# Compression network's first layer of a two-block transformer kernel: split operands and single-pass matmuls

## The chip, the cores and the metric

The kernel runs on one NeuronCore of a Trainium2 chip. Its engines are TensorE (PE: matmuls; PEld: its weight loads), VectorE (DVE), ScalarE (ACT), GpSimd (POOL) and SyncE (SP, which issues most of the DMAs). Each works through its own list of instructions in order, and semaphores tie the lists together. The metric is device time in microseconds of one execution, given as the median of several runs. The profile's clock of the trace starts at the span's start; all times below of the form 383.3 are on it.

## What is computed

Two blocks of a transformer in float32 on 512 tokens of width 1024: a hybrid attention layer, then a layer with "native sparse attention", a gated MLP mixer and a feed-forward part. The change touches one piece of the second block, the network that compresses keys and values:

```python
def compress_tokens(t, pos_emb, w1, w2):            # t [B,G,S,dh], w1 [2048, 256], w2 [256, 64]
    ...
    chunks = t.reshape(B, G, n_chunks, CMP_STRIDE, dh)
    blocks = jnp.concatenate([chunks[:, :, i:i + n_cmp] for i in range(r)], axis=3)
    blocks = (blocks + pos_emb).reshape(B, G, n_cmp, CMP_BLOCK * dh)
    return jax.nn.gelu(blocks @ w1) @ w2
...
kc = compress_tokens(heads_kv(k_c), cmp_pos_k, cmp_w1_k, cmp_w2_k)
vc = compress_tokens(heads_kv(v_c), cmp_pos_v, cmp_w1_v, cmp_w2_v)
```

`blocks` has 2 groups x 31 blocks, held as 64 rows, of 32 x 64 = 2048 numbers. The product `blocks @ w1` (64 x 2048 by 2048 x 256), done once for the keys and once for the values, is "the first layer". The result feeds one of three attention branches of the second block.

## The kernel before

**Precision.** A float32 matmul is done by TensorE in several passes. The large products avoid this: each operand is split into a high part (rounded to the type `float32r`, copied by ScalarE) and a low part (the operand minus its high part, subtracted by GpSimd or VectorE), and three single-pass matmuls high x high, high x low and low x high replace one float32 matmul. The weights of these products arrive in `RAW`, and their two parts go into a ring `WR` of six slots. For each slot, step `split`, ScalarE copies the high part (L1859), then GpSimd subtracts the low part in two halves (L2756). A split stands four slots ahead of the matmuls that use it. The first layer, in contrast, is done in plain float32: `blocks` (64 columns) is the stationary operand, a row block of `w1` (128 x 256) the moving one, 16 such products for the keys and 16 for the values, each in two halves of 8, the steps `hidden 0,0`, `hidden 0,1` (keys) and `hidden 1,0`, `hidden 1,1` (values).

**Stages around it.** The input product of the second block, `in2`, is done in five chunks of columns (408, 512, 384, 512, 512 wide). Each chunk takes 8 weight slots, and for each slot TensorE does four token tiles of three matmuls (L1360). Each token tile has its own PSUM bank, and the chunk's result is copied out of the four banks by ScalarE (tiles 0 and 2) and VectorE (tiles 1 and 3), both L1031, before the next chunk may write there. Between these matmuls stand small steps:

- `qt` (L1627): transposes of one token tile into the one PSUM bank `TR`. All users of `TR` share it, so each must wait until the one before has been copied out. `qt cmp` feeds `cmpT`, from which VectorE forms `blocks` with the position embedding added (L2510, 8 instructions); `qt q` feeds `qS` (ScalarE L1925, then VectorE L2350); `qt slc` transposes `k_nat` and feeds `kS_slc` (ScalarE L1931, VectorE L2365).
- `hidden` (L1753), whose result ScalarE turns through GELU into `hid_nat` (L2061); `hid_t` (L1762) transposes that through `TR` into `hidT` or `hidV`; `cmpkv` (L1770, L1773) is the second layer, from which VectorE forms `kcS` and `vbd` (L2529 to L2534); `CS` (L1784) are the first attention scores, which need them.

**Order.** The lists of all engines come from one timeline. It is written by `make_timeline` from the table `PLAN`, which says before which quarter of a weight slot (one token tile, three matmuls) a step may stand; `follows` names what must have gone before it, `lags` the least distance, and `rank` the order of steps due at the same quarter. Every engine takes from the timeline, in order, what is its own.

## Time and profile before

| | us |
|---|---|
| median of 3 runs (964.64 to 964.97) | 964.74 |
| the profiled execution | 964.92 |
| its span | 962.7 |
| TensorE busy | 946.2 (98%) |
| the four halves of the first layer on TensorE, 3.60 each | 14.4 |

The profiled execution's time lies 2.2 us over its span and 0.2 us over the median. The chain of waits gives TensorE 90% of the span. TensorE's granted clock is 1.00 (2.4 GHz) in the stages from 352 to 418.

### The profile page before, as it was taken

What the parts mean: (1) busy time and instruction counts of PE and PEld (TensorE: products, weight loads), DVE (VectorE), ACT (ScalarE), POOL (GpSimd) and SP (SyncE); (2) the same over time, 40 slices, a digit from 0 to 9 for tenths busy, and PEclk for the clock granted to TensorE, in tenths of its full rate; (3) what the DMA queues carried; (4) which work ended last, traced back from release to release, by engine and by line L of the source; (5) the groups of instructions that cost most, each with busy time, mean ns of one, the idle gap of its engine ahead of it and who ended that gap; (6) DMA issues with size and microseconds to landing.
All of it is one profiled execution on the core that took longest, in us unless ns stands there. A gap on an engine that the chain in (4) does not pass through costs nothing.

```text
span 962.7 us, 14693 instructions
## 1 busy us (share of the span) xinstructions
PE 946.2 (98%) x5579; PEld 823.8 (86%) x5579; DVE 569.4 (59%) x1083; ACT 419.7 (44%) x730; POOL 369.0 (38%) x442
## 2 busy tenths in 40 slices
PE   9999999999999999999999999999999999999997
PEld 8878887878888898688888888888999999988886
DVE  2764445388554356384558743888899999711114
ACT  5334325265555263345464633544444444433332
POOL 5771551246435454122223036597000000366561
PEclk9999999999999999999999999999999999999999
DMA  7374243112144252231211112226322442122312
GB/s 234 120 199 99 66 143 99 45 44 66 44 147 160 70 175 66 76 122 45 72 62 65 45 44 89 74 69 213 116 89 89 128 136 88 46 88 91 124 47 88
DMA packets 74758, 93.44 MB, mean 97 GB/s; under 512 B 15332, under 2 KB 53777, under 8 KB 74688
## 3 DMA queue, kind: packets, MB, share of 16 engines
q1 hardware_dynamic: 74256, 91.91, 29.9%
q8 instruction: 45, 0.74, 0.3%
q10 hardware_dynamic: 432, 0.59, 0.2%
q14 instruction: 25, 0.20, 0.1%
HBM read 90.09 MB, written 7.12 MB: 101 GB/s over the span
## 4 chain that ended last, share of the span: by engine, by line
PE 90%; DVE 4%; ACT 2%; issue 2%; DMA 1%; POOL 0%; SPq 0%; DVEq 0%; POOLq 0%; ACTq 0%
PE psum L1360 52%; PE psum L1421 17%; PE psum L1701 6%; PE psum L1661 4%; PE psum L1676 3%; PE psum L1753 1%; PE psum L1487 1%; PE psum L1627 1%; PE psum L1729 1%; PE psum L1743 1%; PE psum L1714 1%; DMA RAW<-in_w_in_dram 1%; PE psum L1640 1%; PE psum L1799 0%; DVE R L2730 0%
## 5 line engine op out<-in xcount | busy, mean ns | idle before, releaser
L1360 PE MATMUL psum<-WR,XT 128*128 128x512 f32 (+3 forms) x1620 | 390.5, 387 | 1.0 <-ACT R L1031 0.7
L2756 POOL TENSOR_TENSOR WR<-RAW,WR 128x256 fp32r<-128x256 f32 (+3 forms) x320 | 259.9, 841 | 321.0 <-ACT WR L1859 320.9
L1360 PEld LDWEIGHTS psum<-WR,XT 128*128 128x128 f32 x1620 | 285.9, 188 | 51.5 <-issue 4.1
L2756 POOL TENSOR_TENSOR WR<-RAW_B,WR 128x256 fp32r<-128x256 f32 x88 | 71.6, 837 | 202.7 <-ACT WR L1859 202.7
L1859 ACT ACTIVATE WR<-RAW 128x512 fp32r<-128x512 f32 (+3 forms) x160 | 93.4, 603 | 83.5 <-PE psum L1360 69.4
L1360 PE MATMUL psum<-WR,TT 128*128 128x512 f32 x528 | 119.9, 389 | 0.0
L1360 PEld LDWEIGHTS psum<-WR,TT 128*128 128x128 f32 x528 | 99.0, 188 | 20.5
L2034 ACT ACTIVATE prob<-prob,st 128x512 f32<-128x512 f32 (+2 forms) x112 | 58.4, 545 | 92.6 <-DVE st L2418 83.5
L1701 PEld LDWEIGHTS psum<-ones_up,probT 128*128 128x128 f32 x536 | 70.7, 191 | 7.1 <-issue 1.3
L1701 PE MATMUL psum<-ones_up,probT 128*128 128x128 f32 x536 | 72.7, 275 | 0.1
L1421 PE MATMUL psum<-TT,WR 128*128 128x256 f32 x576 | 71.7, 283 | 0.0
L1421 PEld LDWEIGHTS psum<-TT,WR 128*128 128x128 f32 x576 | 70.3, 192 | 0.0
L1360 PE MATMUL psum<-XT,WR 128*128 128x512 f32 (+1 forms) x324 | 67.4, 367 | 0.0
L2613 DVE TENSOR_TENSOR TT<-actT,TT 128x512 fp32r<-128x512 f32 x22 | 17.6, 801 | 84.2 <-ACT TT L2090 84.1
L1360 PEld LDWEIGHTS psum<-XT,WR 128*128 128x128 f32 x324 | 56.2, 188 | 10.1 <-DVE XT L2241 0.2
L1859 ACT ACTIVATE WR<-RAW_B 128x512 fp32r<-128x512 f32 x44 | 27.2, 630 | 70.3 <-PE psum L1360 67.8
L2793 POOL TENSOR_TENSOR st<-st 128x8 f32<-128x8 f32 (+2 forms) x27 | 32.5, 1204 | 65.4 <-DVE st L2316 28.9
L1421 PE MATMUL psum<-XT,WR 128*128 128x256 f32 x432 | 54.1, 283 | 0.0
L1421 PEld LDWEIGHTS psum<-XT,WR 128*128 128x128 f32 x432 | 52.9, 192 | 0.1
L1676 PE MATMUL psum<-ident_sb,prob 128*128 128x128 f32 x268 | 43.1, 276 | 1.9 <-DVE probT L1096 1.2
L1096 ACT ACTIVATE probT<-psum 128x512 f32<-128x512 f32 (+2 forms) x52 | 25.2, 485 | 36.0 <-PE psum L1676 35.8
L2241 DVE TENSOR_TENSOR XT<-psum,XT 128x512 fp32r<-128x512 f32 x32 | 21.0, 687 | 30.0 <-ACT XT L1915 30.0
(292 smaller groups left out, 1254.0 us busy)
## 6 DMA issues: line engine op xcount, KB each, us to landing
RAW<-in_w_gate_up_dram SPq DMA_DIRECT2D x28, 512.0 KB, 5.0
RAW<-in_w_in_dram SPq DMA_DIRECT2D x13, 1024.0 KB, 5.2
RAW_B<-in_w_down_dram SPq DMA_DIRECT2D x11, 1024.0 KB, 5.0
RAW<-in_w_out_dram SPq DMA_DIRECT2D x8, 1024.0 KB, 5.3
RAW_B<-in_w_gate_up_dram SPq DMA_DIRECT2D x16, 512.0 KB, 6.0
RAW<-in_w_in_dram SPq DMA_DIRECT2D x13, 512.0 KB, 4.9
rep_scratch<-rows_scratch SPq DMA_DIRECT2D x12, 320.0 KB, 6.6
RAW<-in_w_in_dram SPq DMA_DIRECT2D x4, 768.0 KB, 4.3
```

Source lines behind the costliest of these rows:

```text
L1096: (eng.activation(dst, src, ACT.Copy) if eng is nc.scalar else eng.tensor_copy(dst, src)).then_inc(tr_out, 1)
L1360: last = pe.matmul(outp, stationary(x), moving(y), start=start and n == 0, stop=stop and n == 2)
L1421: last = pe.matmul(bank[:, 256 * m:256 * m + 256], w[:, k, y, P * m:P * m + P], x_[:, k, z, :], start=fresh and (k, m, y, z) == (0, 0, 0, ...
L1661: last = pe.matmul(bank[:, col:col + m * P], q_of(name, h)[:, P * i:P * i + P], k_of(name, h, x)[:, P * j:P * (j + m)], start=x == 0, stop ...
L1676: last = pe.transpose(TR[:, P * q:P * q + P], buf[:, P * q:P * q + P], ident[:, :])
L1701: last = pe.matmul(OB[:, P * i:P * i + P].rearrange("p (x n) -> p x n", x=2), probT[:, at_:at_ + P], ones_and_v(name, h, j + b), start=b = ...
L1859: act.activation(WR[:, s % RING, 0, 0:w], (DOWN_RAW if s >= first["down", 0] else RAW)[:, raw_half[g], q, 0:w], ACT.Copy).then_inc(w_hi, 1)
L2034: last = act.activation(buf[:, col:col + m * P], buf[:, col:col + m * P], ACT.Exp, bias=nm[:, sl + n:sl + n + 1], scale=-1.0)
L2241: dve.tensor_tensor(XT[:, 4 * hf:4 * hf + 4, 1, P * t:P * t + P], (MM[i] if kind_ == "mm" else XB[i]).rearrange("p (q n) -> p q n", q=4), ...
L2613: dve.tensor_tensor(AT[:, kt % 8, 1, :], actT[:, kt, :], AT[:, kt % 8, 0, :].bitcast(F32), ALU.subtract).then_inc(act_lo, 1)
L2756: last = pool.tensor_tensor(WR[:, s % RING, 1, lo:hi], raw[:, raw_half[g], q, lo:hi], WR[:, s % RING, 0, lo:hi].bitcast(F32), ALU.subtract)
L2793: pool.tensor_tensor(dst, src, half[:, 0:1].broadcast_to([P, n]) if n > 1 else half[:, 0:1], ALU.pow).then_inc(r_ready, 1)
```

## The change

1. **Matmuls.** `blocks` is split too, into `block_parts[kv]` with 64 high and 64 low columns side by side: one stationary operand of 128 columns. Each row block of `w1` is split into `hi_of_w1` and `w1_lo`. For each of the 32 row blocks there are two single-pass matmuls, with the high and the low part of `w1` as the moving operand of 256 columns. PSUM rows 0 to 63 then hold the product with the high part of `blocks`, rows 64 to 127 the one with its low part.
2. **Adding the halves.** ScalarE copies rows 64 to 127 to `hid_nat`, VectorE adds rows 0 to 63, and ScalarE applies GELU. Before, ScalarE applied GELU straight from PSUM.
3. **Splitting `w1`.** 16 new steps `w1`, each for a pair of row blocks: ScalarE copies 128 x 512 high parts, GpSimd subtracts the low parts, in place over `w1`, in two pieces of 256 columns. Pairs 0 to 7 (keys) are due at quarters 16 to 37 of `in2`, pairs 8 to 15 (values) at quarters 62 to 69. Pair 8 and pair 10 wait until the first and the second half of `block_parts` are done, pair 12 until `hidden 0,0` is.
4. **Splitting `blocks`.** Two new steps `bp`: ScalarE copies 128 x 1024 high parts, VectorE subtracts. Keys and values signal apart.
5. **Places.** `hidden` moves from quarters 64, 65, 67, 69 to 64, 66, 69, 72; `hid_t` from 67, 72 to 69, 75; `qt cmp` from 41 to 39 and `blocks` from 55 to 53; `cmpkv` stays at 70, subject to what it follows. The keys' `w1` is now loaded first (in the place and at the time of the values' before), the values' second. Buffers are moved for the new tiles.

```diff
     if kind == "hidden":
         kv, part = at
-        return [("hidden", kv, 0)] if part else [("hidden", 0, 1)] if kv else [("blocks",)]
+        out = [("w1", 4 * (2 * kv + part) + 3)]
+        return out + ([("hidden", kv, 0)] if part else [("hidden", 0, 1)] if kv else [("blocks",), ("bp", 1)])
...
                     if part == 0:
                         wait_sc(step)
-                        pe.wait_ge(s_w1[kv], 16)
-                        pe.wait_ge(blk_done, 1)
+                        pe.wait_ge(blk_done, kv + 1)
+                    pe.wait_ge(w1_lo_done, 4 * (2 * kv + part) + 4)
                     for m in range(8 * part, 8 * part + 8):
-                        last = pe.matmul(SC[nth["hidden", kv, 0] % 2][0:64, 0:256], blocks[:, kv, m, :], w1[kv][:, m, :],
-                                         start=m == 0, stop=m == 15)
-                    if part:
-                        last.then_inc(sc_in, 1)
+                        for x, moving in enumerate((hi_of_w1(16 * kv + m), w1_lo[kv][:, m, :])):
+                            last = pe.matmul(SC[nth["hidden", kv, 0] % 2][:, 0:256], block_parts[kv][:, m, :, :].rearrange("p x n -> p (x n)"), moving,
+                                             start=(m, x) == (0, 0), stop=(m, x) == (15, 1))
+                    last.then_inc(sc_in if part else w1_used, 1)
...
+                elif what == "w1":
+
+                    pair = step[1]
+                    kv, m = divmod(2 * pair, 16)
+                    act.wait_ge(s_w1[kv], 16)
...
+                    if pair in (8, 10):
+                        act.wait_ge(blk_done, pair // 2 - 3)
+                    if pair == 12:
+                        act.wait_ge(w1_used, 1)
+                    act.activation(hi_of_pair(pair), w1[kv][:, m:m + 2, :], ACT.Copy).then_inc(w1_hi_done, 1)
...
                 elif what == "hidden" and step[2]:
                     kv = step[1]
                     act.wait_ge(sc_in, nth["hidden", kv, 0] + 1)
-                    if kv == 0:
-                        act.wait_ge(tr_in, nth["qt", "cmp", 3] + 1)
-                    act.activation(hid_nat[0:64, kv, :], SC[nth["hidden", kv, 0] % 2][0:64, 0:256], ACT.Gelu_apprx_tanh).then_inc(hid_act, 1)
+                    act.activation(hid_nat[0:64, kv, :], SC[nth["hidden", kv, 0] % 2][64:128, 0:256], ACT.Copy).then_inc(hid_low, 1)
+
+                    act.wait_ge(sc_out, nth["hidden", kv, 0] + 1)
+                    act.activation(hid_nat[0:64, kv, :], hid_nat[0:64, kv, :], ACT.Gelu_apprx_tanh).then_inc(hid_act, 1)
...
+                if what == "w1":
+                    pair = step[1]
+                    kv, m = divmod(2 * pair, 16)
+                    pool.wait_ge(w1_hi_done, pair + 1)
+                    for e in range(2):
+                        last = pool.tensor_tensor(w1_lo[kv][:, m + e, :], w1[kv][:, m + e, :], hi_of_pair(pair)[:, e, :].bitcast(F32), ALU.subtract)
+                    last.then_inc(w1_lo_done, 1)
```

The change moves instructions at three places that matter below (line numbers of the changed kernel are up to 59 higher).

ScalarE, end of chunk 0 of `in2`, before:

```order
L1859 ACTIVATE WR<-RAW 128x408
L1859 ACTIVATE WR<-RAW 128x512 x4
L1031 ACTIVATE cmp_nat<-psum,st 128x4x64
L1031 ACTIVATE k_nat<-psum,st 128x2x64
```

The same place after, where `w_hi_...<-w_k` are the copies of the pairs 0 to 5:

```order
L1889 ACTIVATE WR<-RAW 128x408
L2098 ACTIVATE w_hi_b<-w_k 128x512
L1889 ACTIVATE WR<-RAW 128x512
L2098 ACTIVATE w_hi_b<-w_k 128x512
L1889 ACTIVATE WR<-RAW 128x512
L2098 ACTIVATE w_hi_a<-w_k 128x512
L1889 ACTIVATE WR<-RAW 128x512
L2098 ACTIVATE w_hi_a<-w_k 128x512 x2
L1889 ACTIVATE WR<-RAW 128x512
L2098 ACTIVATE w_hi_a<-w_k 128x512
L1061 ACTIVATE cmp_nat<-psum,st 128x4x64
```

Six copies now stand ahead of the one that frees chunk 0's first PSUM bank (`cmp_nat`).

ScalarE, from the high part of the values' blocks to the third `qS`, before (`nat_92` frees a bank of chunk 1):

```order
L1031 ACTIVATE nat_92<-psum,st 128x512 x2
L1925 ACTIVATE qS<-psum 64x4x128 x2
L1859 ACTIVATE WR<-RAW 128x384
L1925 ACTIVATE qS<-psum 64x4x128 x2
L2061 ACT_TABLE_LOAD
L2061 ACTIVATE hid_nat<-psum 64x256
L1925 ACTIVATE qS<-psum 64x4x128 x2
```

The same place after:

```order
L2105 ACTIVATE block_parts_v<-blocks 128x16x64
L2098 ACTIVATE w_hi_d<-w_v 128x512 x2
L1061 ACTIVATE nat_92<-psum,st 128x512 x2
L1955 ACTIVATE qS<-psum 64x4x128 x2
...
L2098 ACTIVATE w_hi_a<-w_v 128x512
L2109 ACTIVATE hid_nat<-psum 64x256
L2112 ACT_TABLE_LOAD
L2112 ACTIVATE hid_nat<-hid_nat 64x256
L1955 ACTIVATE qS<-psum 64x4x128 x2
```

Three instructions came ahead of the bank's copy, and the table load, which stood ahead of the wait for TensorE, now stands behind the copy that has this wait.

TensorE, from the last half of the first layer to the first scores, before:

```order
L1627 MATMUL psum<-ident_sb,k_nat 128x128 x2
L1360 MATMUL psum<-WR,XT 128x384 x6
L1627 MATMUL psum<-ident_sb,k_nat 128x128 x2
L1360 MATMUL psum<-WR,XT 128x384 x3
L1762 MATMUL psum<-ident_sb,hid_nat 128x64 x2
L1360 MATMUL psum<-WR,XT 128x384 x6
L1770 MATMUL psum<-hidT,w2k 128x64 x2
L1773 MATMUL psum<-w2v,hidV 128x64 x4
L1360 MATMUL psum<-WR,XT 128x384 x3
L1627 MATMUL psum<-ident_sb,k_nat 128x128 x2
L1360 MATMUL psum<-WR,XT 128x384 x6
L1784 MATMUL psum<-kcS,qS 128x64 x8
```

The same place after (the first row is two steps of two transposes each, back to back):

```order
L1657 MATMUL psum<-ident_sb,k_nat 128x128 x4
L1390 MATMUL psum<-WR,XT 128x384 x9
L1657 MATMUL psum<-ident_sb,k_nat 128x128 x2
L1792 MATMUL psum<-ident_sb,hid_nat 128x64 x2
L1390 MATMUL psum<-WR,XT 128x384 x6
L1800 MATMUL psum<-hidT,w2k 128x64 x2
L1803 MATMUL psum<-w2v,hidV 128x64 x4
L1814 MATMUL psum<-kcS,qS 128x64 x8
```

The large matmuls that stood between steps which hand `TR` or `kcS` on to one another have moved away from between them.

## Rows read from the trace of the kernel before

**Rows 1.** The page: busy time, share of the span, instructions of each engine.

```profile
PE 946.2 (98%) x5579; PEld 823.8 (86%) x5579; DVE 569.4 (59%) x1083; ACT 419.7 (44%) x730; POOL 369.0 (38%) x442
```

**Rows 2.** Chain of waits, 330 to 430: start, us, what stands on the chain.

```profile
358.89 6.39 PE psum L1360 x27
...
382.86 0.44 PE psum L1627 x4
383.30 3.60 PE psum L1753 x16
...
404.35 0.39 ACT kS_slc L1931
404.84 0.43 DVE kS_slc L2365
...
405.65 1.26 PE psum L1360 x6
...
407.30 0.91 PE psum L1773 x8
...
410.57 1.06 PE psum L1784 x8
```

**Rows 3.** Chain of waits, 700 to 712, where single-pass matmuls of 256 columns run.

```profile
699.94 12.12 PE psum L1421 x101
```

**Rows 4.** Timeline of ScalarE, 346 to 364: start, duration, instruction [idle before, releaser].

```profile
352.37 2.66 ACT L1859 ACTIVATE WR<-RAW 128x408 fp32r<-128x408 f32 x5
357.20 0.47 ACT L1031 ACTIVATE cmp_nat<-psum,st 128x256 f32<-128x256 f32 x1 [2.16 <-PE psum L1360]
```

**Rows 5.** DMAs: issue of the second w1, and (all DMAs by line) its us to landing.

```profile
340.29 0.37 SPq L1267 DMA_DIRECT2D w_k<-in_cmp_w_k_dram  x1
...
w_k<-in_cmp_w_k_dram SPq DMA_DIRECT2D x1, 2048.0 KB, 9.9
```

**Rows 6.** Timeline of GpSimd, 300 to 400.

```profile
353.74 6.78 POOL L2756 TENSOR_TENSOR WR<-RAW,WR 128x204 fp32r<-128x204 f32 x10
...
374.90 1.15 POOL L2756 TENSOR_TENSOR WR<-RAW,WR 128x192 fp32r<-128x192 f32 x2 [2.04 <-ACT WR L1859]
378.11 1.39 POOL L2756 TENSOR_TENSOR WR<-RAW,WR 128x192 fp32r<-128x192 f32 x2 [2.06 <-ACT WR L1859]
```

**Rows 7.** Timeline of VectorE, 376 to 412: the blocks.

```profile
377.15 0.57 DVE L2510 TENSOR_TENSOR blocks<-cmpT,st 128x248 f32<-128x248 f32 x1
...
377.63 1.46 DVE L2510 TENSOR_TENSOR blocks<-cmpT,st 128x248 f32<-128x248 f32 x2
...
380.31 1.07 DVE L2510 TENSOR_TENSOR blocks<-cmpT,st 128x248 f32<-128x248 f32 x2
```

**Rows 8.** Groups by line and shape: count | busy us, mean ns | idle before.

```profile
L2674 DVE TENSOR_TENSOR WR<-formed,WR 128x1024 fp32r<-128x1024 f32 x24 | 29.3, 1222 | 5.3 <-ACT WR L1881 5.1
...
L1881 ACT ACTIVATE WR<-formed 128x1024 fp32r<-128x1024 f32 x24 | 25.4, 1059 | 22.9 <-PE psum L1421 13.7 <-PE psum L1360 8.0 <-DVE formed L2668 1.2
```

**Rows 9.** Timeline of all engines, 352 to 418: one `qS`, and the GELU of the keys.

```profile
382.22 0.69 ACT L1031 ACTIVATE nat<-psum,st 128x512 f32<-128x512 f32 x1 [0.67 <-PE psum L1360]
...
383.33 1.19 ACT L1925 ACTIVATE qS<-psum 64x512 fp32r<-64x512 f32 x2 [0.43 <-PE psum L1627]
...
384.63 1.39 DVE L2350 SCALAR_TENSOR_TENSOR qS<-psum,qS 64x512 fp32r<-64x512 f32 x2 [0.98 <-ACT qS L1925]
...
389.31 1.28 ACT L2061 ACT_TABLE_LOAD   x1
...
391.69 0.38 ACT L2061 ACTIVATE hid_nat<-psum 64x256 f32<-64x256 f32 x1 [1.10 <-PE psum L1753]
```

**Rows 10.** Waits, 376 to 416: engine, line, for whom: us, times, longest.

```profile
PE psum L1784 <- DVE vbd L2534: 0.5, 1, 0.5
PE psum L1762 <- DVE kS_slc L2365: 0.5, 1, 0.5
...
PEld psum L1627 <- DVE kS_slc L2365: 0.3, 1, 0.3
```

More of the change, by code:

```diff
@@ L301, in make_timeline @@
         "OS": 1.5, "CS_b": 1.5, "F": 2, "sp_b": 2.5, "S": 3, "Z": 3, "sp": 4, "qt": 4.5,
-        "gx": 4.2, "xt": 4.4, "blocks": 5, "hidden": 6, "hid_t": 6.5, "gelu": 6, "cmpkv": 7, "gm_w": 8, "gm_a": 9, "gm": 10,
+        "gx": 4.2, "xt": 4.4, "blocks": 5, "bp": 5.2, "w1": 5.5, "hidden": 6, "hid_t": 6.5, "gelu": 6, "cmpkv": 7, "gm_w": 8, "gm_a": 9, "gm": 10,
     }
@@ L461, in make_timeline @@
         on(PLAN["hidden"][n], ("hidden", n // 2, n % 2))
+    for n in range(2):
+        on(PLAN["bp"][n], ("bp", n))
+    for pair in range(16):
+        on(PLAN["w1"][pair], ("w1", pair))
     for n in range(2):
@@ L997, in ones_and_v, with hi_of_w1, hi_of_pair @@
             return ones_up[:, 0:2 * at_].rearrange("p (x n) -> p x n", x=2)[:, :, 0:HD]
+        def hi_of_w1(n):
+            part, slot = ((1, 0), (0, 0), (0, 4), (2, 0), (3, 0), (3, 4), (0, 0), (0, 4))[n // 4]
+            return w1_hi[part][:, slot + n % 4, :]
+        def hi_of_pair(pair):
+            part, slot = ((1, 0), (0, 0), (0, 4), (2, 0), (3, 0), (3, 4), (0, 0), (0, 4))[pair // 2]
+            return w1_hi[part][:, slot + 2 * pair % 4:slot + 2 * pair % 4 + 2, :]
         def bias_of(name, h, i, m):
@@ L1258, in load_w1 @@
             def load_w1(kv):
-                if kv:
+                if not kv:
                     sp.wait_ge(tr_in, nth["F", 3, 2] + 1)
```

51 lines of the change are left out of this document (41 added, 10 removed).

## Prediction

> **What bounds the kernel now.** I read the busy line first: TensorE is busy 98% of the span [rows 1], so what leaves TensorE's list gains, and what makes TensorE wait costs, nearly one for one. Then the chain of waits around the first layer [rows 2]: each of the four halves of the first layer (L1753 x16) is on it with 3.60 us, and between 403 and 411 it leaves TensorE for short handovers through VectorE and ScalarE. Then the timelines of the three engines to which the change gives work [rows 4, 6, 7, 9], for where they have room. Everything up to the end of chunk 0 of `in2` and everything after the scores keeps its order, so the difference arises between 353 and about 417.
>
> **What TensorE saves.** Before, 4 x 3.60 = 14.4 us. After, each half has 16 single-pass matmuls of 256 columns with a stationary operand of 128 columns. The same shape runs elsewhere at 12.12 / 101 = 0.120 us [rows 3], so a half takes 1.92 us: 4 x 1.68 = 6.7 us saved. The Trainium skill (TensorE: Matmul & The Clock Gate, "Back-to-back issue gap") gives N/2.4 + 2.5 ns, 109 ns for 256 columns; by it 0.7 us more would be saved, but the row has this kernel's own spacing, and the sum goes by that.
>
> **What the change adds, in order of the program.** Between engines I allow 0.06 us for each handover.
>
> (a) *ScalarE before chunk 1.* Before, ScalarE ends a burst of five copies at 355.0 (2.66 us, 0.53 each), then idles 2.16 us until chunk 0's first bank is full at 357.20 [rows 4]; TensorE's chunk 1 starts at 358.89, when that bank is copied out [rows 2]. Now six copies of `w1` pairs stand in this burst: 6 x 0.53 = 3.2 us against 2.16 idle. ScalarE reaches the bank 1.0 late, and TensorE with it: **+1.0** (0.8 to 1.3). The keys' `w1` is no wait here: even the second load, issued at 340.29, lands 9.9 us later [rows 5], and the keys' is now the first.
>
> (b) *ScalarE, then VectorE, in chunk 1.* Two more copies come ahead of the gates' exponential, which VectorE needs before it may empty `TR` after the first `qt cmp`; the second `qt cmp` then waits a little: **+0.3** (0 to 1.0). Chunk 1 now ends at 382.86 [rows 2] + 1.3 = 384.2.
>
> (c) *First `qt q`, behind the blocks.* Before, GpSimd is idle for most of the time in which VectorE forms the blocks; only one split lies beside them, at 378.11, and it stretches from 1.15 to 1.39 [rows 6], while the pair of blocks instructions at 377.63 takes 1.46 against 1.07 for the pair at 380.31 [rows 7]. With the pair after it, that one split costs VectorE 0.7 us. Now GpSimd has eight `w1` pairs at 2 x 0.71 = 1.42 (the burst from 353.74 has eight pieces of 256 columns and two of 204 in 6.78 [rows 6]), 11.4 us, and runs without a gap from 353.74: chunk 1's last split ends near 377.7, and four splits of chunk 2 follow, all beside the blocks. The blocks start at 377.1 again (1.3 later by a and b, 1.4 earlier since `qt cmp` stands two quarters ahead), take eight times 0.5 alone and 4 x 0.7 for the splits: done at 384.0. Then, in a row: VectorE's subtract for the keys, 1.22 [rows 8], for which pair 8 waits on ScalarE; two copies of pairs, 1.07; the copy of chunk 1's first bank, 0.69 [rows 9]; the transposes. That is 387.0 with handovers, against 384.2 when TensorE is there: **+2.8**. The ends: with one split beside the blocks, as before, they are done at 381.9 and the wait is 0.7; with VectorE at half speed all the time and a little more for its two subtracts, 3.6. I take 2.8 since the only rows with both engines at it say so. What is queued on VectorE behind this is the second bank of chunk 1, needed only after the first half of the layer.
>
> The Trainium skill (SBUF — State Buffer, "SBUF: two separate sides") has a rule against this change: GpSimd and a VectorE instruction with two SBUF inputs share one port pair, and who comes second is held for the other's whole instruction. Each of the eight GpSimd pieces would then hold VectorE by its full 0.575 instead of the 0.35 that the rows show: (c) would be 4.6 instead of 2.8 and the whole forecast 1.8 us later.
>
> (d) *Second `qt q`.* Its `TR` must be emptied: ScalarE 1.19, VectorE 1.39 [rows 9], 2.7 with handovers. TensorE has a half (1.92) and three matmuls (0.6) for it: **+0.2** (0 to 0.5).
>
> (e) *Fourth `qt q`.* Its list is now: second half for the keys, 3 matmuls, third `qt q`, 6 matmuls, fourth `qt q`, which waits until the third is out of `TR`. On ScalarE, ahead of emptying the third, stand the low rows' copy, which waits for that half, the table load and the GELU. From the half's end: 0.38 + 1.28 + 0.38 + 1.19 (ScalarE), 1.39 (VectorE) [rows 9], 4.8 with handovers. TensorE meanwhile has 9 matmuls of 384 columns (six take 1.26 [rows 2]), 1.9, and four transposes, 0.44: **+2.4** (1.8 to 2.8). Before, the table load was over at 390.6, before the half ended [rows 9].
>
> (f) *`hid_t` of the keys* waits for the fourth `qS`, 2.7, with only a half, 1.92, to cover it: **+0.8** (0.5 to 1.2).
>
> (g) *Two `qt slc` back to back* after the last half. The second waits until ScalarE has copied the low rows (0.38), VectorE has added (0.4), ScalarE has done GELU (0.38) and its part of `kS_slc` (0.39), and VectorE its part (0.43 [rows 2]): 2.3 with handovers, less the first one's own 0.4, 1.9. Six matmuls covered this before, and 0.3 was left [rows 10]: **+1.6** (1.2 to 1.9).
>
> (h) *`hid_t` of the values* directly behind the third `qt slc`: 0.39 + 0.43 and handovers, 1.0; before, three matmuls covered it and 0.5 was left [rows 10]: **+0.5** (0.3 to 0.7).
>
> (i) *First scores directly behind `cmpkv`.* From the end of `cmpkv` at 407.30 + 0.91 to the scores at 410.57 are 2.36 us of VectorE forming `kcS` and `vbd` [rows 2]. Before, nine matmuls and two transposes lay in them and 0.5 was left as a wait [rows 10]; now nothing lies there: **+1.8** (1.6 to 2.0).
>
> The GpSimd pieces themselves I cost at nothing on top: without contention, chunk 1's fourth slot is ready at 367.7 and needed at 369.5, its last at 377.7 and needed at 381.3. That cover is thin, and its loss is the rival B. The final order of the DMAs (the t5 biases follow the last half) moves with TensorE and is not waited for.
>
> **Sum.** -6.7 + 1.0 + 0.3 + 2.8 + 0.2 + 2.4 + 0.8 + 1.6 + 0.5 + 1.8 = **+4.7 us**. All low ends together give +0.2, all high ends +8.3. On the profiled execution's 964.92 that is 969.6, on the median, 0.2 less, **969.4**. So the single passes save what they promise, and more than that is spent in handovers whose covering matmuls have been thinned out.
>
> **Rivals.**
>
> *A: the saving shows (faster).* The waits (d) to (i) all hang on one point: that nothing stands between the emptying of `TR` and its next user. If TensorE's queue and the engines behind it close these gaps as they did before, when four `qt q` cost no wait at all, only (a), (b) and the low end of (c) remain: -6.7 + 1.0 + 0.3 + 0.7 = -4.7, 960.0. With (c) at 0.7, the kernel is faster by more than can be told from no change as soon as (d) to (i) together come to under 2.8 us. Before, the same handovers left 0.3 to 0.5 each [rows 10], which speaks for it; but there matmuls lay between, and the printed order has none. 0.08.
>
> *B: GpSimd falls behind (slower still).* If each piece costs GpSimd what the contended split shows (1.39 for 1.15, a fifth more [rows 6]), nine groups of pieces up to chunk 1's fourth slot bring 2.7 us and the slot comes 0.9 late; sixteen groups up to the last slot bring 4.8, and it comes 1.2 late; TensorE waits for `WR` in chunk 1. +4.7 + 1.2 = +5.9, 970.6. Most of that time VectorE works from PSUM, beside which the splits kept their pace, so 0.14.
>
> *C: half of it.* The blocks are not held up (c at 0.7) and (e) falls to half, since ScalarE's list is shorter than I make it: +1.4, 966.1, within 0.2%. 0.12.
>
> *D: the change does not do what it says,* that is, a matmul of 128 stationary and 256 moving columns here takes longer than 0.120, say the 0.225 of a sixteenth of a half before (3.60 / 16): no saving, and only (d) and (f), which a half covers, fall away: 11.4 - 1.0 = +10.4, 975.1. The same types and shape are in rows 3, so 0.02.
>
> **How the numbers follow.** The forecast gets 0.64, and its own range is 967.0 to 971.8. The range for 8 in 10 leaves out A and the upper end of B and D, and takes in most of C: 965.6 to 972.2. A measurement of this kernel can tell about 0.2%, 1.9 us, from no change: slower is above 966.7, faster below 962.8. Slower: the forecast, B, D and nothing of C, less a margin for terms that I may have counted twice, 0.78. Same: C and that margin, 0.13. Faster: 0.09.
>
> **What would show it.** In the profile of the changed kernel the halves should be 1.9 us each on the chain; chunk 1 should start near 359.9; TensorE should idle before the first `qt q` (2 to 3 us, behind VectorE's blocks instructions of 0.7 to 0.9 us instead of 0.57), before the fourth (2.4, VectorE's `qS`), before the second `k_nat` pair (1.9) and before the first scores (2.3). If the idle stands before L1390 with GpSimd as the releaser, it is B; if TensorE is still gapless, A. I am wrong outright if the chain shows fewer than 5 us of new waits between 353 and 417.

## The result, and the profile after

| | before | after |
|---|---|---|
| median, us | 964.86 | 987.52 (987.19 to 987.81) |
| profiled execution's span, us | 962.7 | 986.0 |
| TensorE busy, us | 946.2 (98%) | 949.3 (96%) |

The ratio is 1.0235, with a 95% interval of 1.0217 to 1.0253: the change makes the kernel 22.7 us slower. The direction was forecast, the size was not: 969.4 with a range up to 972.2. No rival comes near it either.

The page of the kernel after, its busy line (it answers to [rows 1]) and two lines of the span in 40 slices of 24.65 us:

```profile
PE 949.3 (96%) x5579; PEld 831.9 (84%) x5579; DVE 584.5 (59%) x1087; ACT 430.8 (44%) x750; POOL 392.8 (40%) x474
...
PE   9999999999999985789999999999999999999997
...
PEclk9999999999999997969999999999999999999999
```

TensorE is no longer busy throughout: four slices, from 345 to 444 us, show only some 80%, 50%, 70% and 80%, and in the second and the fourth of them the granted clock is well below full speed too. Its timeline there, with the idle time ahead of a row and who ended it in brackets (rows of the large product lie between):

```profile
359.82 4.55 PE L1390 MATMUL psum<-WR,XT 128*128 128x512 f32 x19 [0.94 <-ACT st L1061]
...
379.80 1.12 PE L1657 MATMUL psum<-ident_sb,cmp_nat 128*128 128x128 f32 x4 [11.76 <-DVE cmpT L2412]
380.57 4.15 PE L1390 MATMUL psum<-WR,XT 128*128 128x512 f32 x12
...
384.91 3.00 PE L1390 MATMUL psum<-WR,XT 128*128 128x512 f32 x12
...
397.98 0.63 PE L1657 MATMUL psum<-ident_sb,nat 128*128 128x128 f32 x4 [0.74 <-issue]
...
401.40 0.66 PE L1657 MATMUL psum<-ident_sb,nat 128*128 128x128 f32 x4 [0.34 <-DVE qS L2401]
...
409.40 0.66 PE L1657 MATMUL psum<-ident_sb,nat 128*128 128x128 f32 x4 [2.85 <-DVE qS L2401]
...
419.66 0.44 PE L1657 MATMUL psum<-ident_sb,k_nat 128*128 128x128 f32 x2 [2.09 <-DVE kS_slc L2416]
...
423.93 0.47 PE L1792 MATMUL psum<-ident_sb,hid_nat 64*128 64x64 f32 x2 [1.00 <-DVE kS_slc L2416]
...
431.45 1.89 PE L1814 MATMUL psum<-kcS,qS 128*128 128x64 f32 x8 [2.38 <-DVE vbd L2593]
```

The second line is half of the story: the second `qt cmp` waits 11.76 us. The first layer itself is as forecast where the clock is full: in the first half of the keys the 16 matmuls stand 0.120 us apart (398.69, 398.81, 398.93 and so on), 1.92 us. The third half, behind the wait of 2.85 us, takes 3.1. The releaser, VectorE's copy of `cmpT`, was not slow. It stood behind this:

```profile
364.88 12.31 DVE L2598 TENSOR_SCALAR st<-st 128x96 f32<-128x96 f32 x1 [3.96 <-ACT st L2128]
...
378.02 0.42 DVE L2409 COPY cmpT<-psum 64x256 f32<-64x256 f32 x1
```

L2598 adds 1 to 96 numbers per partition, a step on the way to the branch gates, and takes 12.31 us. GpSimd's timeline in that time, the first and the last of its rows:

```profile
363.39 2.82 POOL L2834 TENSOR_TENSOR w_k_lo<-w_k,w_hi_a 128x256 fp32r<-128x256 f32 x4
...
374.37 2.76 POOL L2815 TENSOR_TENSOR WR<-RAW,WR 128x256 fp32r<-128x256 f32 x4
```

GpSimd subtracts low parts from 353.87 without a pause, and its run ends at 377.13. VectorE's instruction ends at 377.19. The other half of the story is the clock. Stretches of the span: length, busy us (and number of instructions) of PE, PEld, DVE, ACT and POOL, granted clock, share and GB/s of the DMAs:

```profile
379.00:382.00 3.00, 2.20 (x8) 1.92 (x9) 1.75 (x5) 0.00 (x0) 0.00 (x0) 0.50 0.63 230
...
409.00:413.00 4.00, 3.60 (x20) 3.47 (x20) 1.72 (x3) 2.25 (x5) 4.00 (x7) 0.66 0.00 0
...
423.00:432.00 9.00, 5.70 (x23) 5.42 (x23) 3.30 (x12) 2.04 (x3) 1.14 (x2) 0.50 1.01 365
432.00:440.00 8.00, 8.00 (x40) 7.90 (x40) 4.04 (x11) 0.80 (x2) 0.00 (x0) 0.65 0.03 10
```

0.50 is the lower level, 1.2 GHz. Here it stands behind the longer waits: the first 12 matmuls behind the 11.76 us take 4.15 us, 12 of the same shape at 384.91 take 3.00.

**The account** of the 23.3 us of span: the eight waits above are 22.1 us, less 1.0 that stood at two of these places before [rows 10], less the 6.7 saved, is 14.4. The remaining 8.9 are put down to the clock. This is what is left over, not a measurement; an estimate bears it out: busy time times what is missing to 1.00, over the stretches from 379 to 440, is about 10 us (TensorE's busy time is not all bound by its clock). Up to 352 the stages of the two kernels agree, and the last 522.7 us have the same number of matmuls and 514.5 us of TensorE's work in both, so nothing was lost elsewhere.

### The profile page after: what moved, and what is told of

It reads as the page before. It is cut to its first block, busy times and chain, and to the rows that moved or that the text cites. A ratio compares the mean times of both kernels' runs of the same rounds, so it can differ in the third digit from the quotient of the medians.

```text
span 986.0 us, 14751 instructions
## 1 busy us (share of the span) xinstructions
PE 949.3 (96%) x5579; PEld 831.9 (84%) x5579; DVE 584.5 (59%) x1087; ACT 430.8 (44%) x750; POOL 392.8 (40%) x474
## 4 chain that ended last, share of the span: by engine, by line
PE 56%; DVE 4%; ACT 2%; issue 1%; POOL 0%; DVEq 0%; POOLq 0%; ACTq 0%
PE psum L1390 30%; PE psum L1451 16%; PE psum L1731 3%; PE psum L1691 2%; PE psum L1706 2%; DVE st L2598 1%; PE psum L1784 1%; PE psum L1657 1%; PE psum L1517 1%; DVE R L2789 0%; PE psum L1814 0%; DVE qS L2401 0%; PE psum L1846 0%; ACT WR L1889 0%; ACT w_hi_a L2098 0%
## 5 line engine op out<-in xcount | busy, mean ns | idle before, releaser
L1390 PE MATMUL psum<-WR,XT 128*128 128x512 f32 (+3 forms) x1620 | 394.7, 390 | 1.8 <-ACT st L1061 0.9
L1390 PEld LDWEIGHTS psum<-WR,XT 128*128 128x128 f32 x1620 | 289.6, 191 | 52.0 <-issue 4.1
```

The source lines that it names most:

```text
L1390: last = pe.matmul(outp, stationary(x), moving(y), start=start and n == 0, stop=stop and n == 2)
```

## The experiments

The kernel before was run beside each of them, with medians from 964.8 to 965.0. Where a kernel ran once, its one time is given. The executions of one changed kernel scatter by up to 7.1 us (e10) where those of before scatter by at most 0.7, so single microseconds are read from the profiled executions. "The +1" is L2598's addition; the letters (L, S, Q, R and so on) are the theories of the expectations.

**e1: a pause for VectorE.** GpSimd waits, ahead of pair 5, until the +1 is done.

```diff
                     link(dve.tensor_scalar(g_tmp, g_tmp, 1.0, None, ALU.add))
+                    dve.sem_inc(gates_added, 1)
...
                 if what == "w1":
...
+                    if pair == 5:
+                        pool.wait_ge(gates_added, 1)
```

> The changed kernel, but GpSimd waits, before the low parts of pair 5, until VectorE's addition for the gates (L2598 in the changed kernel, 12.31 us there) is done. Theory L (port): this one-input SBUF instruction is held for as long as GpSimd's subtractions follow one another without a pause, so it ends when GpSimd pauses at 367.6: 2.7 us instead of 12.3, the second `qt cmp` waits 2 us instead of 11.8, time 973 to 976. Theory D (VectorE's own): the 12.3 us come from something at VectorE or ScalarE and not from GpSimd's run; then GpSimd waits with it, and the time is 987 or more.

973.68 us. Timeline of VectorE, then of GpSimd:

```profile
364.51 2.80 DVE L2599 TENSOR_SCALAR st<-st 128x96 f32<-128x96 f32 x1 [3.96 <-ACT st L2129]
```

```profile
365.82 1.43 POOL L2817 TENSOR_TENSOR WR<-RAW,WR 128x256 fp32r<-128x256 f32 x2
367.52 1.41 POOL L2838 TENSOR_TENSOR w_k_lo<-w_k,w_hi_a 128x256 fp32r<-128x256 f32 x2 [0.27 <-DVEq L2600]
```

The +1 ends at 367.31, 0.06 behind the end of the piece ahead of the pause. A pause of 0.27 us is worth 13.8 us.

**e2: the +1 with two inputs.** The same value from an instruction that reads `g_tmp` twice, max(x + 1, x).

```diff
-                    link(dve.tensor_scalar(g_tmp, g_tmp, 1.0, None, ALU.add))
+                    link(dve.scalar_tensor_tensor(out=g_tmp, in0=g_tmp, scalar=1.0, in1=g_tmp, op0=ALU.add, op1=ALU.max))
```

> The changed kernel, but the addition for the gates is a form with two SBUF inputs (x+1 as max(x+1, x)) in place of one with one input. Theory L: forms with two SBUF inputs take turns with GpSimd (the blocks of the kernel before: 0.57 became 0.93), so it lasts under 1.5 us, and the time is what was forecast without this stall, 968 to 974. Rival L2: every VectorE instruction that needs SBUF beside GpSimd is held until the run ends: 12 us again, 987.

986.37 (983.38 to 987.88), ratio 1.0226 (1.0209 to 1.0243). Timeline of VectorE:

```profile
364.41 12.37 DVE L2598 SCALAR_TENSOR_TENSOR st<-st 128x96 f32<-128x96 f32 x1 [3.95 <-ACT st L2128]
```

Held as long, to 376.78, 0.12 behind GpSimd's end. One input from SBUF or two makes no difference for the +1, and the expected 968 to 974 fell.

**e3: no low parts for the keys.** GpSimd leaves the keys' eight pairs out, and the second matmul of each row block takes the high part again, so that TensorE's work is the same and the keys' first layer is computed with another operand.

```diff
+                    if pair < 8:
+                        pool.sem_inc(w1_lo_done, 1)
+                        continue
```

> The changed kernel without GpSimd's 16 subtractions for the keys (the second matmul of each row block takes the high part again, so the low part of the keys' weights is left out of the result; the number and shape of matmuls stay). Theory L: GpSimd pauses before and while the gates are added, the addition lasts under 1 us, time 967 to 973. Theory D: 12.3 us and 987, since ScalarE's copies and VectorE's list are unchanged.

971.09. Timeline of VectorE:

```profile
364.56 0.21 DVE L2598 TENSOR_SCALAR st<-st 128x96 f32<-128x96 f32 x1 [3.96 <-ACT st L2128]
```

0.21 us is what the +1 takes when it is let in at once. The second `qt cmp` waits for nothing, and 16.4 us are back. In the kernel before the same instruction took 0.73, beside pieces of GpSimd: the sign was there, in a trace that I had read for other lines. Timelines of VectorE, GpSimd and ScalarE of the kernel before:

```profile
363.10 0.73 DVE L2539 TENSOR_SCALAR st<-st 128x96 f32<-128x96 f32 x1 [2.31 <-ACT st L2077]
```

```profile
360.93 4.23 POOL L2756 TENSOR_TENSOR WR<-RAW,WR 128x256 fp32r<-128x256 f32 x6 [0.42 <-ACT WR L1859]
```

```profile
362.87 0.62 ACT L1859 ACTIVATE WR<-RAW 128x512 fp32r<-128x512 f32 x1
```

It ended at 363.83, inside a row of six pieces of 256 columns without a pause. "What stays open" returns to this.

**e4: the kernel before, low parts of chunk 1 in pieces of 64 columns**, eight to a split.

```diff
-                    for lo, hi in ((0, w // 4 * 2), (w // 4 * 2, w)):
+                    pieces = [(64 * e, 64 * e + 64) for e in range(8)] if first["in2", 1] <= s < first["in2", 1] + 8 else ((0, w // 4 * 2), (w // 4 * 2, w))
+                    for lo, hi in pieces:
```

> The kernel before, with nothing of the change, but GpSimd's splits of chunk 1 of `in2` in eight pieces of 64 columns instead of two of 256. A piece should cost 0.33 us (0.21 + 0.0019 per column, from pieces of 130 to 256 columns), a slot 2.7, and GpSimd then runs without a pause from 355 to about 376, while each slot is still ready before TensorE needs it. Theory L: the addition for the gates (0.73 us before) is held to about 376, 12 to 13 us, the kernel before becomes 12 to 18 us slower, 977 to 983. Theory D: 0.7 us and 965.

964.62: no loss. Timeline of GpSimd, then of VectorE:

```profile
353.89 22.57 POOL L2757 TENSOR_TENSOR WR<-RAW,WR 128x204 fp32r<-128x204 f32 x72
```

```profile
363.24 0.43 DVE L2539 TENSOR_SCALAR st<-st 128x96 f32<-128x96 f32 x1 [2.30 <-ACT st L2077]
```

GpSimd runs for 22.57 us without a pause, as after, and yet VectorE gets in within 0.43. An unbroken run alone is not the cause, and the expectation fell. Two things differ from the kernel after: the width of the pieces, and everything else that the change brought. The next two runs part them.

**e5 and e6: the kernel before, with nothing changed but more for GpSimd to do** in chunk 1, in pieces of 256 and of 128 columns. The extra low parts go into free memory. e5's lines are below; in e6 all pieces of chunk 1 have 128 columns, two extra and four real ones to a split.

```diff
+                    n = s - first["in2", 1]
...
+                    if 0 <= n < 8:
+                        for e in range(2):
+                            part, at_ = (0, 2 * n + e) if n < 4 else (1 + (n - 4) // 2, 2 * (n % 2) + e)
+                            pool.tensor_tensor(spare[part][:, at_, :], RAW[:, raw_half[g], q, 256 * e:256 * e + 256], WR[:, s % RING, 0, 256 * e:256 * e + 256].bitcast(F32), ALU.subtract)
```

> The kernel before, in which GpSimd subtracts each of the eight low parts of chunk 1 of the second projection twice, the extra one (two pieces of 256 columns, ahead of the real ones) into memory that nothing reads. No other engine has anything new to do, and TensorE's order is that of before. At 0.70 us a piece (the 6.78 for 10 of [rows 6]) the 32 pieces are 22.5 us, a run from about 354 to 376 us as in the kernel after, in pieces of the same width. Theory L (VectorE's +1 for the gates, which reads and writes SBUF, is held as long as GpSimd's pieces of 256 columns follow each other with no pause): the +1 takes over 8 us and up to 13, TensorE's second turn of the compression queries waits for it, and the time is 975 to 983. Rival M (the 12.31 us come from something else that the change brought: ScalarE's copies of the key weights, their transfer, or the places in memory): the +1 takes 0.4 to 1.5 us, and the time is 964 to 967, the most being what chunk 1 loses to low parts that come later.

> The same in pieces of 128 columns: per split of chunk 1 two extra ones ahead of four real ones, 48 in all. In the run with pieces of 64 columns a piece took 0.31 us, in [rows 6] one of 256 took 0.70, so one of 128 is estimated at 0.44 and the run at 21 us without a pause. Theory S (the width of a piece decides: where a piece is short enough, VectorE comes in at a boundary): either the +1 takes 0.4 to 1.0 us as with 64 columns, and the limit lies between 128 and 256, or it takes over 8 us, and the limit lies between 64 and 128. Rival Q (not the width, but whether the next piece stood ready already decides): here as with 64 columns all pieces of a split stand ready, so the +1 takes under 1 us here and over 8 us in the run with 256 columns only if the width matters too; a value between, of 2 to 6 us, would say that VectorE waits for the end of a split. Time 964 to 967 where it is short.

e5 978.33, e6 974.43. Timeline of VectorE in e5, of GpSimd in e5, of VectorE in e6 and of GpSimd in e6:

```profile
362.89 15.18 DVE L2540 TENSOR_SCALAR st<-st 128x96 f32<-128x96 f32 x1 [2.23 <-ACT st L2078]
```

```profile
375.51 2.48 POOL L2765 TENSOR_TENSOR WR<-RAW,WR 128x256 fp32r<-128x256 f32 x4
```

```profile
363.23 10.83 DVE L2540 TENSOR_SCALAR st<-st 128x96 f32<-128x96 f32 x1 [2.28 <-ACT st L2078]
```

```profile
373.44 2.85 POOL L2765 TENSOR_TENSOR WR<-RAW,WR 128x128 fp32r<-128x128 f32 x6
```

In e5 the +1 ends at 378.07, GpSimd's run at 377.99. Neither ScalarE's copies, nor the transfers, nor the places in memory, nor anything on TensorE is needed to hold VectorE for 15 us: rival M has fallen, and L stands for pieces of 256 columns. With 128 columns it is held too, though it was done at 374.06, 2.2 us ahead of the end of the run at 376.29, for a reason that no row shows. By the expectation the limit would lie between 64 and 128 columns; whether it is the width that decides is tested by e13 below.

**e7: the +1 on ScalarE.** GpSimd's run stays as it is.

```diff
                     act.activation(g_tmp, g_tmp, ACT.Exp, scale=-1.0).then_inc(gate_e, 1)
+                    act.wait_ge(gate_e, 1)
+                    act.activation(g_tmp, g_tmp, ACT.Copy, bias=1.0).then_inc(gate_e, 1)
...
-                    dve.wait_ge(gate_e, 1)
-                    link(dve.tensor_scalar(g_tmp, g_tmp, 1.0, None, ALU.add))
+                    dve.wait_ge(gate_e, 2)
```

> The kernel after with the gates' +1 taken from VectorE: ScalarE adds it behind its Exp (a Copy with bias 1), and VectorE has the reciprocal alone. GpSimd's run is as it was. Theory L1 (only some forms of VectorE's work on SBUF are held: the +1 was in all runs, the reciprocal of 0.75 us ran beside GpSimd in the kernel before): the reciprocal takes about 0.75 us at 365 to 366, the second turn of the compression queries waits for nothing, and the time is that of the run without low parts for the keys, 970.5 to 972.5. Rival L2 (every instruction of VectorE on SBUF alone is held): the reciprocal takes 11 to 12 us, and the time is 985 to 988.

974.08 (973.91 to 978.53), ratio 1.0111 (1.0087 to 1.0135). Timeline of VectorE, then of GpSimd:

```profile
364.85 0.75 DVE L2600 RECIPROCAL st<-st 128x96 f32<-128x96 f32 x1 [4.27 <-ACT st L2130]
...
376.41 4.29 DVE L2563 TENSOR_TENSOR blocks<-cmpT,st 128x248 f32<-128x248 f32 x1
```

```profile
374.14 6.18 POOL L2816 TENSOR_TENSOR WR<-RAW,WR 128x256 fp32r<-128x256 f32 x10
```

The reciprocal, SBUF to SBUF in the middle of GpSimd's run, takes its 0.75 us: not every instruction is held, L2 has fallen for it. But the time missed the expected 970.5 to 972.5, because a second victim came up. GpSimd's run now ends at 380.32, and the first addition of the blocks, 0.57 alone [rows 7], is held to 380.70. The first `qt q` waits 4.13 us: its row names no releaser, but ScalarE reaches the copies of chunk 1's banks only at 386.82, behind its work on the blocks and the pairs. In the kernel after this was hidden, since everything but GpSimd was 12 us late by then.

**e10: three pairs of key weights behind the blocks** instead of ahead of them, on top of e7.

```diff
-'w1': (16, 19, 22, 25, 28, 31, 34, 37, 62, ...), 'bp': (59, 62)
+'w1': (16, 19, 22, 25, 28, 61, 61, 61, 62, ...), 'bp': (59, 60)
```

> The kernel with the +1 on ScalarE (972.1 us of span, first scores at 418.89), in which three of the eight pairs of key weights (5, 6 and 7) are split behind the parts of the blocks instead of ahead of them: GpSimd's run of chunk 1 is 4.3 us shorter (three pairs at 1.43). There the first addition of the blocks, which VectorE reads from SBUF and writes to SBUF, took 4.29 us (376.41 to 380.70) beside a run of GpSimd that ended at 380.32, and the first turn of the queries waited 4.13 us. Theory L (held until GpSimd pauses): the first addition falls to 0.57 to 1.5 us, the wait to 0.7 to 1.5 us, and the time by 2 to 3.5 us, to 970.5 to 972. Rival: the three pairs now run behind the additions and hold what follows them there (the parts of the blocks, or the second half of the keys, which needs these pairs), and the time stays at 973 to 975.

970.89 (970.78 to 977.88), ratio 1.0082 (1.0053 to 1.0111), span 969.1. Timeline of VectorE, then all waits of TensorE from 352 to 470 (in total, times, longest):

```profile
376.06 0.57 DVE L2563 TENSOR_TENSOR blocks<-cmpT,st 128x248 f32<-128x248 f32 x1
```

```profile
PE psum L1657 <- DVE qS L2403: 2.9, 1, 2.9
PE psum L1814 <- DVE vbd L2595: 2.4, 1, 2.4
PE psum L1657 <- issue: 2.1, 1, 2.1
PE psum L1657 <- DVE kS_slc L2418: 2.1, 1, 2.1
PE psum L1829 <- DVE probT L2629: 1.1, 1, 1.1
PE psum L1792 <- DVE kS_slc L2418: 1.0, 1, 1.0
PE psum L1792 <- DVE qS L2403: 0.9, 1, 0.9
PE psum L1390 <- ACT st L1061: 0.4, 1, 0.4
PE psum L1706 <- DVE probT L1126: 0.4, 1, 0.4
```

With both holds gone, this is about the kernel that the forecast described, and these are its terms. Its clock, however, does not follow the length of a wait. Behind the longest one, 2.86 us ahead of the fourth `qt q`, it stays at 1.00, and the 16 matmuls of the third half stand 0.12 us apart:

```profile
397.50:400.20 2.70, 2.57 (x20) 2.37 (x20) 0.65 (x2) 1.93 (x4) 2.70 (x5) 1.00 0.00 0
```

It falls behind the 2.09 us ahead of the first `qt q` (0.55 from 386 to 388.6, where the first half of the keys takes 3.0 us) and behind the 2.37 ahead of the first scores (0.76 from 415.8 to 422.8).

**e12 and e11: the small waits.** e12 loads the GELU table early (a GELU of four numbers behind the gates' step); e11 adds later places for three steps.

```diff
+                    act.activation(hid_nat[64:128, 0, 0:4], ss[64:128, 0:4], ACT.Gelu_apprx_tanh)
...
-'qt_slc': (67, 4), 'cmp': (77, 3, 3, 5, 6), lags[6]: 0
+'qt_slc': (72, 2), 'cmp': (78, 3, 3, 5, 6), lags[6]: 1
```

> The kernel with both holds of VectorE taken away (span 969.1 us), and one edit more: ScalarE loads the GELU table where it is idle, by a GELU of four numbers behind the gates' step, instead of between the copy of the low rows and the GELU of the keys (1.28 us at 393.10), behind which the third turn's copies of the queries queue. Term (e) as forecast: the load is a part of what the fourth turn of the queries waits for (2.86 us at 397.58), so that wait falls to about 1.6 and the time by 1.3 us or somewhat more, to 969 to 969.8, if TensorE's granted clock, which is 1.2 GHz for a while behind that wait, stays higher. Rival: the fourth turn waits for something else next (VectorE's queries' low parts behind the copies), and under 0.5 us is gained.

> The same, and three steps a little later in the order: the second turn of the keys of the second branch two quarters behind the first instead of right behind it (term g: 2.09 us), the third and fourth behind the values' hidden part (h: 1.00), and the first scores one quarter behind the compressed keys and values instead of at once (i: 2.37). TensorE's products are as many and in the same chunks. If these waits are what the forecast said, places in the order that ask for a result before it can be there: the three fall by 1.5, 0.8 and 0.5 us, and the time by 2.5 to 4 us against the run with the table early, to 965.5 to 967.5. Rival, as the two runs with a wider order showed: what follows the first scores bunches, new waits and a lower granted clock take the gain back, and the time is 968 to 972.

e12 971.95 (970.21 to 973.5), ratio 1.0078 (1.0061 to 1.0095), span 968.4; e11 970.36 (969.94 to 975.32), ratio 1.0068 (1.0044 to 1.0093), span 968.1. Neither can be told from e10 by its times. In e12's timeline the fourth `qt q` waits 2.03 instead of 2.86, not the 1.6 expected. The expectation of e12 has the clock at 1.2 GHz for a while behind that wait; in e10's trace, as said above, it is not. Timeline of TensorE in e11:

```profile
406.59 0.44 PE L1657 MATMUL psum<-ident_sb,k_nat 128*128 128x128 f32 x2 [1.03 <-DVE kS_slc L2419]
...
413.96 1.05 PE L1814 MATMUL psum<-kcS,qS 128*128 128x64 f32 x8 [1.80 <-DVE vbd L2596]
...
437.26 1.11 PE L1706 MATMUL psum<-ident_sb,prob 128*128 128x128 f32 x4 [2.30 <-DVE probT L1126]
```

The three waits fall from 2.09, 1.00 and 2.38 to 1.03, 0.47 and 1.80, as the mechanism says (a little less than the expected 1.5, 0.8 and 0.5 in sum), and the first scores start 1.2 us earlier than in e12. Behind them a wait of 2.30 appears where 0.42 stood: the gain is handed back, and the rival of the expectation was right.

**e8 and e9: a wider order.** Turns of the queries three quarters apart, all later steps moved back, fewer pairs ahead of the evictions, the GELU table early (e8, on e7; its main numbers below); much the same with the three late pairs and the Exp table loaded early (e9).

```diff
-'hidden': (64, 66, 69, 72), 'hid_t': (69, 75), 'cmpkv': 70, 'qt_q': (63, 2), 'qt_slc': (67, 4), 'cmp': (77, 3, 3, 5, 6)
+'hidden': (64, 67, 70, 73), 'hid_t': (70, 77), 'cmpkv': 78, 'qt_q': (63, 3), 'qt_slc': (74, 2), 'cmp': (80, 3, 3, 5, 6)
```

> That kernel with the steps behind chunk 1 spread out so that no wait that the forecast named is left: ScalarE copies four pairs of key weights ahead of the evictions instead of six (term a); the turns of the queries stand three quarters apart instead of two (terms c to e), the halves with them; the key turns of the second branch (g), the turn of the values' hidden part (h) and the first scores (i, two quarters behind the compressed keys and values) come later; and ScalarE loads the GELU table behind the gates' Exp by a GELU of four numbers, where it is idle, instead of between two turns. If the terms' cause is what the forecast said (a place in the order too early for what it waits for) the waits of 0.94, 2.85, 2.09, 1.00 and 2.38 us fall to under 0.5 each and the granted clock stays at 1.00: the saving of 6.7 us shows at the place of the first scores, less up to 1.6 us that the 9 matmuls ahead of them moved there cost, and the time is 958 to 964. Rival: the later first scores push what follows them (the compressed branch's softmax, the first head of the next branch) against the end of the projections, and the gain is lost there: 964 to 969. A third: new waits take the place of the old: 969 to 972.

> All the repairs at once: the three late pairs, the +1 on ScalarE, the turns of the queries three quarters apart, the GELU table loaded early, the Exp table loaded behind the last GELU instead of ahead of the compressed branch's first Exp (there the run with the spread order waited 3.12 us for it), and the first scores one quarter behind the compressed keys and values instead of two. The run with the spread order had its first scores at 416.36, of which 3.4 us were the hold of the blocks' addition (4.10 against about 0.7): without it 413, and 2.5 us later than in the kernel before (410.57), though with 3 more matmuls of the projection behind it. If the order behind the first scores is then as tight as before: 965 to 968. If the chains there (scores, ScalarE's Exp, turns) bunch against the third chunk's evictions as in the spread run: 969 to 972. That it beats the kernel before (under 963.5) would need every wait to be gone; the theory gives that a small chance.

e8 976.66 (975.3 to 977.07), ratio 1.0120 (1.0105 to 1.0135); e9 975.56 (974.76 to 977.17), ratio 1.0113 (1.0098 to 1.0128). Both are worse than what they repair, and slower than every range in their expectations. In e8 the waits named fell (0.94 to 0.15 before chunk 1, 2.86 to none before the fourth `qt q`), and others came: 1.07 for GpSimd's low parts of the values, 3.12 for ScalarE's Exp behind the first scores, 1.55, 1.05 and 0.69 after it. e9 is the more telling one: its waits from 352 to 470 sum to 11.3 us, those of e10 to 13.2, and yet its span is 5.4 us longer. Stretches of e9 and of e10:

```profile
412.00:424.00 12.00, 10.69 (x44) 10.12 (x44) 5.39 (x16) 1.21 (x3) 1.42 (x2) 0.50 0.55 207
424.00:440.00 16.00, 16.00 (x90) 15.36 (x89) 13.79 (x46) 4.95 (x10) 3.05 (x5) 0.90 0.00 0
```

```profile
412.00:424.00 12.00, 9.63 (x61) 9.43 (x61) 6.93 (x21) 1.48 (x4) 0.00 (x0) 0.86 0.65 239
424.00:440.00 16.00, 14.49 (x86) 13.06 (x85) 14.40 (x45) 6.62 (x17) 5.72 (x8) 1.00 0.00 0
```

From 412 to 424 e9 has 1.2 GHz throughout and is busy with 44 matmuls; e10 is busy for less time and does 61. Busy time times what is missing to 1.00 is 5.3 + 1.6 us in e9 and 1.3 in e10 (estimates from these rows); over all stretches from 352 to 470 it is 10.7 in e9 and 2.7 in e10. The 8.0 between them, less e9's 1.9 us of shorter waits, is 6.1, near the measured 5.4. Ahead of 412, e9's TensorE had waited 1.57, 2.55 and 0.48 us, but e10's had waited longer (2.86, 0.87, 2.09 and 1.00) and kept its clock. So a sum of waits did not order these two kernels; by the estimate the clock did. Which waits bring the clock down stays open.

**e13: the kernel after, two pairs in pieces of 64 columns,** all else in 256. It asks whether the width of the pieces at that moment decides.

```diff
+                    n = 64 if pair in (4, 5) else 256
                     for e in range(2):
-                        last = pool.tensor_tensor(w1_lo[kv][:, m + e, :], ...)
+                        for x in range(0, 256, n):
+                            last = pool.tensor_tensor(w1_lo[kv][:, m + e, x:x + n], ...)
```

> The kernel after, in which GpSimd splits two of the sixteen pairs of weights (4 and 5) in pieces of 64 columns instead of 256; all else is in pieces of 256 as before, and the run stays without a pause. With pieces of 0.33 us (the mean of 64 in the run with the kernel before) a pair takes 2.6 us instead of 1.4, so pair 4 is split from about 364.8 to 367.4 and the +1 (ready at 364.9) falls into it. Theory S (VectorE comes in between two short pieces): the +1 takes under 1.5 us, the second turn of the compression queries waits for under 1 us, and GpSimd, 2.3 us longer, now holds the first addition of the blocks, as in the run with the +1 on ScalarE (4.3 us there), so that the time is 973 to 977. Rival R (in the run with the kernel before it was not the width of the pieces: what had to be there was that the whole run was short pieces): the +1 is held to the end of GpSimd's run or to the end of pair 4 at the least (2.5 us and up), and the time is 975 to 990.

977.3. Timeline of VectorE, then of GpSimd:

```profile
365.17 4.56 DVE L2598 TENSOR_SCALAR st<-st 128x96 f32<-128x96 f32 x1 [3.96 <-ACT st L2128]
```

```profile
363.69 3.67 POOL L2836 TENSOR_TENSOR w_k_lo<-w_k,w_hi_a 128x256 fp32r<-128x256 f32 x10
367.33 1.41 POOL L2815 TENSOR_TENSOR WR<-RAW,WR 128x256 fp32r<-128x256 f32 x2
368.71 2.30 POOL L2836 TENSOR_TENSOR w_k_lo<-w_k,w_hi_a 128x64 fp32r<-128x64 f32 x8
```

The +1 ends at 369.73, inside the second stretch of short pieces (from 368.71), and took 7.7 us less than in the kernel after. But it was not let in during the first stretch (about 365.1 to 367.3, the last eight of the ten pieces of the first row), so S, under 1.5 us, fell. By the numbers set ahead the result is R's: held beyond the end of pair 4, 2.5 us and up, 975 to 990. Yet R does not say why it was let in at the second stretch, where in the kernel after nothing let it in. One event in one run fits a part for short pieces and does not show it.

**What stays open.** Which boundary lets VectorE in. It got in at one between pieces of 64 columns in e4, 0.43 us with its own 0.21, and at none of the seven or so in e13's first stretch; at one between pieces of 128 columns only after 10.8 us; at one between pieces of 256 in the kernel before, after 0.73 us. So width alone does not decide. A rival is Q, of e6's expectation: whether the next piece stood ready already. In the kernel before, ScalarE finished the high part for the fifth and sixth pieces at 363.49, just ahead of the boundary near 363.75 at which VectorE got in; in the kernel after, ScalarE had finished the last high part that the run needs at 366.70, so that behind it all pieces up to 377.13 stood ready. No run changes this alone, and e4, where the pieces stood ready too, speaks against it as the only condition. That GpSimd's run holds VectorE is shown by the runs; when a run holds it is not.

## Why the prediction failed, step by step

- **The saving, -6.7: right at the clock that it was made for.** Three of the four halves take 1.92 us or a little less in the kernel after; the third takes 3.1 at the lower clock, which the account puts under the clock.
- **Step (b), +0.3 with a range to 1.0: the step that failed.** It cost 11.76 us of waiting and the low clock behind it; with this hold alone taken away (e7) the time falls by 13.4 us. I costed it by ScalarE's two copies ahead of the gates' exponential and priced nothing for VectorE's own instruction, while I wrote a few lines on that GpSimd now "runs without a gap from 353.74". The gates' step, the blocks' additions and the two subtractions for their low parts are the places in this stretch where VectorE works from SBUF to SBUF; the evictions and the `cmpT` copies around them read PSUM. e1, e3, e5 and e7 show the cause from four sides: a pause, no low parts, more low parts in the kernel before, and another engine for the +1.
- **The price of one contention.** In (c) I took 0.35 us of delay per piece from the contended rows [rows 6, 7], and weighed against it the rule of the Trainium skill (SBUF — State Buffer, "SBUF: two separate sides"), by which the loser is blocked for the winner's whole instruction. Both are too small. Rows 6 and 7 have one split with idle time on both sides; in a run the loser stays blocked over 17 instructions and more, 12.31 us here and 15.18 in e5. The same section names VectorE's modes with two ports and forms with two SBUF inputs as those that need the shared pair, and mentions deep queues that would have to be drained to share it. That the additions, with two SBUF inputs, were held (4.29 us in e7) agrees with it; in which mode the +1 and the reciprocal ran no trace shows. The length of the hold is what the section leaves out.
- **(c), +2.8, 0.7 to 3.6:** 0.74 in the kernel after, where the blocks came 12 us late and GpSimd had finished; 4.13 in e7, where they did not, which is outside my range; 2.09 in e10. Right in place, wrong in kind: in e7 one hold to the end of the run, then additions at their own speed, not a slowing of each.
- **The small terms** came near the forecast, net of what stood before. In the kernel after: (a) 0.94 for 1.0; (d) 0.34 for 0.2 (none in e10, where the slow first half covered it). In e10: (e) 2.86 for 2.4; (f) 0.87 for 0.8 (0 in the kernel after, where the slow clock covered it); (g) 2.09 for 1.6; (h) 1.00 less 0.5 for 0.5; (i) 2.38 less 0.5 for 1.8. e11 shows the mechanism of the last three: steps placed later and waits shorter. So rival A, by which these gaps close, fell.
- **The clock: a term that was missing.** All terms were made at 2.4 GHz, since the rows of before had it everywhere from 352 to 440. For e10 the waits up to the first scores, 11.7 less 1.0 before, less 6.7, give +4.0 of span, and +6.4 was measured; from 384 to 400 and from 412 to 424 its clock is 0.89 and 0.86, about 2.7 us by the estimate above. In the kernel after 8.9 us are left for it.
- **The range.** It held e10's time (970.9), the kernel without the holds, and not the kernel at hand. Rival B, that GpSimd falls behind and TensorE waits for `WR`, did not come about: nothing in chunk 1 waits for a low part. What GpSimd's full list did was to lock another engine out while meeting its own dates.

No version beat the kernel before; the best, e11, is 0.7% slower. Within this order the single passes save 6.7 us and the handovers that they uncover, with the clock, cost more.

## What to carry to other kernels

Before GpSimd's list is filled up without gaps, look for each VectorE instruction from SBUF to SBUF that falls into the run, price it at up to the whole rest of the run, and ask who queues behind it. Not every form is held: the reciprocal was not. A wait in the right place (0.27 us on GpSimd), a move to ScalarE, or later work for GpSimd takes such a hold away, and each one taken away may uncover the next. And a wait of TensorE is priced with the slow matmuls that may stand behind it, not by its length alone.

## What the hardware showed that I had not expected

- GpSimd's subtractions held a VectorE instruction of 0.21 us for 12.31 us (after), 12.37 (e2) and 15.18 (e5), up to 0.06 to 0.12 us behind the last of them. Pieces of 128 columns held it for 10.83 us, pieces of 64 for 0.43 in one run and 4.56 in a mixed one.
- Beside the same run the reciprocal took its 0.75 us (e7), and copies and scalings from PSUM their 0.42 and 0.48.
- Behind a wait of 2.85 us TensorE's granted clock fell: of the following 16 matmuls of 256 columns the first stood 0.12 us apart and the later ones, from 410.40 on, 0.21; the stretch has a clock of 0.66. Behind waits of 0.94, 0.74 and 0.34 it stayed at 1.00. In e10 it stayed at 1.00 behind a wait of 2.86 too, at the same place in the order, and fell behind one of 2.09.
